# Feed-forward parts with block sums: the first and third sum of weight blocks by a plain load and an accumulating transfer

## The reference

```python
def _swiglu(x, wg, wu, wd):
    return (jax.nn.silu(x @ wg) * (x @ wu)) @ wd
```

## Time and profile before

| | |
|---|---|
| median of three runs | 1286.71 us (1285.36 to 1286.94) |
| the profiled execution's own time | 1287.52 us |
| its span, from the first to the last instruction | 1285.8 us |
| PE busy | 1268.0 us, 99% of the span |
| DVE busy | 909.5 us, 71% |
| ACT busy | 717.7 us, 56% |
| POOL busy | 130.6 us, 10% |
| moved by transfers | 252.84 MB, mean 197 GB/s |

### The profile page before, as it was taken

One profiled execution on the slowest core, in us unless ns is written; L12 is line 12 of the kernel. 1 busy time (PEld: TensorE's weight loads), 2 busy tenths in 40 slices (PEclk: granted clock), 3 DMA queues, 4 the chain that ended last, 5 costly groups with the idle time before them and its releaser, 6 DMA issues.

```text
span 1285.8 us, 17821 instructions
## 1 busy us (share of the span) xinstructions
PE 1268.0 (99%) x6941; PEld 1049.8 (82%) x6941; DVE 909.5 (71%) x1016; ACT 717.7 (56%) x952; POOL 130.6 (10%) x120
## 2 busy tenths in 40 slices
PE   8999999999999999999999999999999999999998
PEld 6887788888888888877788887888887887788886
DVE  4487776554876665766887866878866687887874
ACT  4344544445755555746746556555647655746553
POOL 3000099000450000020000000000000200000000
PEclk9999999999999999999999999999999999999999
DMA  9997486556465555562766354946264544675351
GB/s 336 351 402 243 141 284 215 192 185 208 127 224 181 187 191 195 192 209 66 254 206 228 98 189 155 327 132 229 82 229 132 165 147 132 219 272 188 108 175 70
DMA packets 164853, 252.84 MB, mean 197 GB/s; under 512 B 9336, under 2 KB 119220, under 8 KB 164788
## 3 DMA queue, kind: packets, MB, share of 16 engines
q1 hardware_dynamic: 161792, 243.28, 56.6%
q0 software_dynamic: 2624, 8.48, 1.7%
q10 hardware_dynamic: 372, 0.19, 0.1%
HBM read 248.73 MB, written 1.05 MB: 194 GB/s over the span
## 4 chain that ended last, share of the span: by engine, by line
PE 88%; ACT 5%; DVE 4%; SPq 1%; DMA 1%; issue 1%; DVEq 0%; ACTq 0%
PE ps L757 19%; PE ps L759 18%; PE ps L758 18%; PE ps L864 10%; PE ps L861 5%; PE ps L975 3%; PE ps L976 3%; PE ps L979 3%; PE ps L805 1%; PE ps L1362 1%; PE ps L797 1%; PE ps L798 1%; DMA raw<-in_conv_w_in 1%; PE ps L781 1%; ACT xT_pair L1611 1%; PE ps L1225 1%
## 5 line engine op out<-in xcount | busy, mean ns | idle before, releaser
L2171 DVE TENSOR_TENSOR w_lo<-raw,w_hi 128x2048 fp32r<-128x2048 f32 x150 | 344.0, 2298 | 92.9 <-ACT w_hi L1548 92.2
L1548 ACT ACTIVATE w_hi<-raw 128x2048 fp32r<-128x2048 f32 x150 | 285.9, 1910 | 117.9 <-PE ps L759 83.0
L757 PE MATMUL ps<-w_lo,hT_hi 128*128 128x512 f32 x400 | 157.0, 393 | 0.2
L864 PE MATMUL ps<-xT_pair,w_hi 128*128 128x512 f32 x576 | 157.2, 394 | 0.0
L758 PE MATMUL ps<-w_hi,hT_hi 128*128 128x512 f32 x400 | 155.9, 390 | 0.0
L759 PE MATMUL ps<-w_hi,hT_lo 128*128 128x512 f32 x400 | 155.8, 389 | 0.0
L757 PE MATMUL ps<-w_lo,xT_pair 128*128 128x512 f32 x356 | 141.5, 398 | 0.0
L759 PE MATMUL ps<-w_hi,xT_pair 128*128 128x512 f32 x356 | 138.9, 390 | 0.0
L758 PE MATMUL ps<-w_hi,xT_pair 128*128 128x512 f32 x356 | 138.7, 390 | 0.0
L864 PEld LDWEIGHTS ps<-xT_pair,w_hi 128*128 128x128 f32 x576 | 98.4, 189 | 13.2
L757 PE MATMUL ps<-xT_pair,w_hi 128*128 128x256 f32 x368 | 108.4, 294 | 0.2 <-DVE xT_pair L2577 0.2
(11 more groups left out here) (345 smaller groups left out, 2260.1 us busy)
## 6 DMA issues: line engine op xcount, KB each, us to landing
raw<-in_ffn_w_down SPq DMA_DIRECT2D x88, 512.0 KB, 4.4
raw<-in_ffn_w_gate SPq DMA_DIRECT2D x64, 512.0 KB, 4.0
raw<-in_ffn_w_up SPq DMA_DIRECT2D x64, 512.0 KB, 5.0
raw<-in_ffn_w_in SPq DMA_DIRECT2D x44, 512.0 KB, 4.6
raw<-in_conv_w_in SPq DMA_DIRECT2D x24, 512.0 KB, 9.9
arena<-in_ffn_w_up SPq DMA_DIRECT2D x24, 512.0 KB, 5.7
raw<-in_fox_w_in SPq DMA_DIRECT2D x24, 512.0 KB, 4.6
raw<-in_ffn_w_out SPq DMA_DIRECT2D x22, 512.0 KB, 4.1
```

Of the source, the lines that this page charges most:

```text
L757: pe.matmul(o, a_hi, b_lo, start=first, stop=False, skip_group_check=True)
L864: mm = pe.matmul(ps[:, bank, :].rearrange("p (s c) -> p s c", s=2), hi[:, cols[k]], xT_pair[:, :, 4 * u + k, :], start=False, stop=u == 1 ...
L1548: act.activation(w_hi[:, slot_of(n), :], raw[:, raw_slot(n), :], ACT.Copy).then_inc(hi_ready, 1)
L2171: dve.tensor_tensor(w_lo[:, slot_of(n), :], source(n), w_hi[:, slot_of(n), :].bitcast(F32), ALU.subtract).then_inc(raw_done, 1)
```

## The change

T1 and T3 are no longer formed by DVE. For T1 SP loads b_12 (the up columns) plainly into the buffer that becomes T1, and when it has landed, POOL issues a transfer of the gate block from the chip's main memory that adds to what is there. For T3 SP loads b_12 into a second buffer, and POOL issues a transfer that adds b_22. b_11, b_22 and b_21 are still loaded plainly. So a pair has five plain block loads (`L_X` and `L_Y` under T1 and T3, and `L_B22`, `L_B21`, `L_B11`) in place of four, and two accumulating transfers. `L_B11` comes last. T1 has a buffer of its own in `arena` (before: `tmp`), and two small buffers move. The semaphores of the four old block loads and of the sums are replaced or count anew.

```diff
-        b_11, b_12, b_22 = part(0, SLOT), part(2048, SLOT), part(4096, SLOT)
+        b_11, b_12, b_22, t_1 = [part(0 + i * SLOT, SLOT) for i in range(4)]
         b_21 = rows_flat[:, 2048:4096]
-        t_1, t_2 = [b[:, :, :].rearrange("p t d -> p (t d)") for b in (tmp, xn)]
+        t_2 = xn[:, :, :].rearrange("p t d -> p (t d)")
...
-                    dst = (b_11, b_12, b_22, b_21)[i].rearrange("p (k c) -> p k c", k=4)
-                    wd, k0 = ((gate, 0), (up, 0), (up, 4), (gate, 4))[i]
+                    dst = {L_B11: b_11, L_B22: b_22, L_B21: b_21, L_X: t_1, L_Y: b_12}[i].rearrange("p (k c) -> p k c", k=4)
+                    wd, k0 = {L_B11: (gate, 0), L_B22: (up, 4), L_B21: (gate, 4), L_X: (up, 0), L_Y: (up, 0)}[i]
...
                 sp.wait_ge(x_new, x_count(s - 1, 1, 1))
-                block(0, 0)
+                block(L_X, 0)
                 half_chunk(6, 2, 1)
-                block(1, 0)
+                block(L_Y, 0)
                 down_rows(7, 1)
-                block(2, 0)
+                block(L_B22, 0)
                 half_chunk(8, 3, 0)
-                block(3, 0)
+                block(L_B21, 0)
                 half_chunk(9, 3, 1)
+                block(L_B11, 0)
                 down_rows(10, 2)
                 down_rows(15, 3)
                 chunk(19, 6)
-                sp.wait_ge(raw_done, n + 13)
-                block(0, 1)
+                sp.wait_ge(raw_done, n + 15)
+                block(L_X, 1)
                 down_rows(21, 4)
                 sp.wait_ge(raw_done, n + 17)
-                block(1, 1)
+                block(L_Y, 1)
                 sp.wait_ge(raw_done, n + 18)
-                block(2, 1)
+                block(L_B22, 1)
                 sp.wait_ge(raw_done, n + 19)
-                block(3, 1)
+                block(L_B21, 1)
+                block(L_B11, 1)
                 down_rows(23, 5)
...
-                    act.wait_ge(sum_ok, 4 * i + {Q_T1: 1, Q_T2: 2, Q_T3: 3, Q_T4: 4}[q])
+                    act.wait_ge(sum_ok, 2 * i + (1 if q == Q_T2 else 2))
...
-                def sum_first(p):
-                    dve.wait_ge(quad_landed[0], 64 * (pair_no(s, p) + 1))
-                    if p:
-                        dve.wait_ge(raw_done, n + 14)
-                    else:
-                        dve.wait_ge(yT_ok, sums_count(s) + 1)
-                    dve.tensor_tensor(t_1, b_11, b_12, ALU.add).then_inc(sum_ok, 1)
...
                 def sum_second(p):
-                    dve.wait_ge(quad_landed[1], 32 * (pair_no(s, p) + 1))
-                    dve.wait_ge(sum_ok, 4 * pair_no(s, p) + 1)
+                    dve.wait_ge(t1_landed, sum_count(s, p))
+                    dve.wait_ge(block_landed[L_B22], block_count(s, p))
...
-                def sum_third(p):
-                    dve.wait_ge(sum_ok, 4 * pair_no(s, p) + 1)
-                    dve.tensor_tensor(b_12, b_12, b_22, ALU.add).then_inc(sum_ok, 1)
...
+            def add_blocks(s, p):
+
+                gate, up, _ = ffn_weights(s)
+                c0 = QUAD_CHUNK[p] * FCH
+                for plain, summed, dst, src in ((L_X, t1_landed, t_1, gate[:, 0:4, c0:c0 + 512]), (L_Y, t3_landed, b_12, up[:, 4:8, c0:c0 + 512])):
+                    pool.wait_ge(block_landed[plain], block_count(s, p))
+                    pool.dma_start(dst.rearrange("p (k c) -> p k c", k=4), src, accum_op=ALU.add).then_inc(summed, 16)
+
+            for s in (FFN2, FFN3):
+                for p in range(2):
+                    add_blocks(s, p)
             for i in range(FOX_H // 2):
...
+            for p in range(2):
+                add_blocks(FFN4, p)
```

More of the change, by code:

```diff
@@ L67 @@
            {22: Q_B21, 24: Q_B11, 25: Q_T1, 26: Q_T2, 28: Q_T3, 29: Q_B22, 30: Q_T4})
+L_B11, L_B22, L_B21, L_X, L_Y = range(5)
 QUAD_CHUNK = (4, 7)
@@ L286, in block_program @@
             "p (b h s) -> p b h s", b=2, h=2)
-        b_11, b_12, b_22 = part(0, SLOT), part(2048, SLOT), part(4096, SLOT)
+        b_11, b_12, b_22, t_1 = [part(0 + i * SLOT, SLOT) for i in range(4)]
         b_21 = rows_flat[:, 2048:4096]
-        t_1, t_2 = [b[:, :, :].rearrange("p t d -> p (t d)") for b in (tmp, xn)]
+        t_2 = xn[:, :, :].rearrange("p t d -> p (t d)")
         quad_src = {Q_B21: b_21, Q_B11: b_11, Q_T1: t_1, Q_T2: t_2, Q_T3: b_12, Q_B22: b_22, Q_T4: b_21}
-        s_1, u_2 = part(6144, 512), part(6656, 512)
+        s_1 = part(8192, 512)
+        u_2 = soft[:, :, :].rearrange("p a b -> p (a b)")
         s_5, u_3 = rows[:, 0, 0:512], rows[:, 0, 512:1024]
@@ L307, in block_program @@
         par_landed = sem("par_landed")
-        quarter_landed = [[sem(f"quarter_landed{q}{a}") for a in range(2)] for q in range(4)]
+        block_landed = [sem(f"block_landed{i}") for i in range(8)]
+        t1_landed = sem("t1_landed")
+        t3_landed = sem("t3_landed")
         part_landed = [sem(f"part_landed{i}") for i in range(NSLOT)]
@@ L369, in block_program @@
         up_tok0 = sem("up_tok0")
-        quad_landed = [sem(f"quad_landed{i}") for i in range(3)]
         e_ok = sem("e_ok")
@@ L457, in pair_no, with block_count, sum_count @@
             return 2 * SEVEN.index(s) + p
+        def block_count(s, p):
+            return 32 + 32 * (pair_no(s, p) + 1)
+        def sum_count(s, p):
+            return 16 * (pair_no(s, p) + 1)
         def row_count(s, c):
@@ L586, in block @@
                 def block(i, p):
-                    dst = (b_11, b_12, b_22, b_21)[i].rearrange("p (k c) -> p k c", k=4)
-                    wd, k0 = ((gate, 0), (up, 0), (up, 4), (gate, 4))[i]
+                    dst = {L_B11: b_11, L_B22: b_22, L_B21: b_21, L_X: t_1, L_Y: b_12}[i].rearrange("p (k c) -> p k c", k=4)
+                    wd, k0 = {L_B11: (gate, 0), L_B22: (up, 4), L_B21: (gate, 4), L_X: (up, 0), L_Y: (up, 0)}[i]
                     c0 = QUAD_CHUNK[p] * FCH
                     for h in (0, 2):
-                        sp.dma_start(dst[:, h:h + 2, :], wd[:, k0 + h:k0 + h + 2, c0:c0 + 512]).then_inc(quad_landed[max(i - 1, 0)], 16)
+                        sp.dma_start(dst[:, h:h + 2, :], wd[:, k0 + h:k0 + h + 2, c0:c0 + 512]).then_inc(block_landed[i], 16)
                 chunk(0, 0)
@@ L635, in load_quarter @@
                     for s in range(2):
-                        sp.dma_start(quarter_raw[q][a][:, :, s, :], ada_1[:, 4 * a:4 * a + 4, s, q * QUARTER:(q + 1) * QUARTER])                            .then_inc(quarter_landed[q][a], 16)
+                        sp.dma_start(quarter_raw[q][a][:, :, s, :], ada_1[:, 4 * a:4 * a + 4, s, q * QUARTER:(q + 1) * QUARTER])                            .then_inc(block_landed[2 * q + a], 16)
             def load_mod(q):
@@ L1135, in quarter_sums @@
             def quarter_sums(q, a):
-                pe.wait_ge(quarter_landed[q][a], 32)
+                pe.wait_ge(block_landed[2 * q + a], 32)
                 for g in range(4):
@@ L1756, in quad_hi @@
                 if q in (Q_B11, Q_B22, Q_B21):
-                    act.wait_ge(quad_landed[{Q_B11: 0, Q_B22: 1, Q_B21: 2}[q]], (64 if q == Q_B11 else 32) * (i + 1))
+                    act.wait_ge(block_landed[{Q_B11: L_B11, Q_B22: L_B22, Q_B21: L_B21}[q]], block_count(s, p))
+                elif q in (Q_T1, Q_T3):
+                    act.wait_ge(t1_landed if q == Q_T1 else t3_landed, sum_count(s, p))
                 else:
-                    act.wait_ge(sum_ok, 4 * i + {Q_T1: 1, Q_T2: 2, Q_T3: 3, Q_T4: 4}[q])
+                    act.wait_ge(sum_ok, 2 * i + (1 if q == Q_T2 else 2))
                 act.wait_ge(w_used, n - NSLOT + 1)
@@ L2453, in sum_second @@
                     dve.tensor_tensor(t_2, t_1, b_22, ALU.add).then_inc(sum_ok, 1)
-                def sum_third(p):
-                    dve.wait_ge(sum_ok, 4 * pair_no(s, p) + 1)
-                    dve.tensor_tensor(b_12, b_12, b_22, ALU.add).then_inc(sum_ok, 1)
                 def sum_fourth(p):
-                    dve.wait_ge(sum_ok, 4 * pair_no(s, p) + 2)
+                    dve.wait_ge(sum_ok, 2 * pair_no(s, p) + 1)
                     dve.wait_ge(raw_done, n + (23 if p else 12))
@@ L2494, in seven @@
                 turned(1, 2)
-                sum_first(0)
                 lo(8)
@@ L2501, in seven @@
                 turned(2, 0)
-                sum_third(0)
                 lo(11)
@@ L2515, in seven @@
                 lo(20)
-                sum_first(1)
                 turned(4, 3)
@@ L2522, in seven @@
                 turned(5, 0)
-                sum_third(1)
                 lo(24, 25, 26)
```

## The result

| | median of the runs | lowest to highest | profiled execution | its span |
|---|---|---|---|---|
| before, measured beside it | 1285.57 us (6 runs) | 1285.36 to 1286.94 | | |
| changed | 1307.55 us (6 runs) | 1305.06 to 1313.88 | 1306.50 us | 1304.7 us |

The changed kernel is slower: the ratio is 1.0167, with a 95% interval from 1.0153 to 1.0182, some 21.5 us. The sign and the mechanism are the predicted ones; the loss is a little over twice the predicted 9.9 us.

What follows compares the result with a forecast made beforehand. PE was taken as the bound, DVE's freed time worth 0; 3 x (2.8 + 0.5) = 9.9 us on the profiled 1287.52 gave 1297.4, less 0.81 to the median, 1296.6 us. Range 1285.5 to 1304, the forecast's own 1290 to 1304.

Steps and rivals of the forecast that it cites:

- the sum 3 x (2.8 + 0.5): Three FFN parts, each losing 2.8 us in pair 0 and 0.5 in pair 1: 9.9 us slower.
- c: Price of one accumulating transfer in plain 1 MB loads of 2.83 us: taken as 1.75, margins used up from 1.25.
- pair 1's 0.5: Loss per part ahead of the columns that need b_21 (unit 22): 0.5 us, range 0 to 1.0.
- What bounds the kernel: In the three changed parts PE sets the pace; taking 27.4 us of sums from DVE gains 0.
- The full stretch: From 624 to 652 us, at pair 0's block loads, DMA engines are full: mean share 1.05 at 371 GB/s.
- 5.66 c - 7.1: Pair 0's loss per part: landings of units 8 to 10 delayed 5.66 c, less a 7.1 us margin; 2.8 us.
- The shift of landings: Pair 0: both accumulating transfers are served before unit 8 lands, so units 8 to 10 land 5.66 c later.
- the rival *same time: No change, 1286.7 us: c below 1.4, or accumulating transfers give way to ring loads until units 8 to 10; chance 0.37.
- The sign that the prediction named: PE gap of 2 to 4 us ahead of unit 8 in each part, released by DVE's split of it.
- The margins of pair 0: Delay PE can stand from landing to need: unit 8 7.1 us, unit 9 7.1, unit 10 7.3 behind b_11.
- b_21's limit as 706.5: Pair 1: b_21 must land by 706.5 for PE's need at 709.82, landing near 699.5 before: margin 7.0 us.
- The upper bound: All three parts at c = 2 with 1.0 us for pair 1: 3 x 5.2 = 15.6 us, 1302.3 us.

Runs made afterwards that it cites:

- e4: The kernel before without DVE's sums for T1 and T3 and with nothing in their place: 1286.91 us, ratio 0.9999.
- e2: The changed kernel without POOL's transfers, T1 and T3 left as their plain blocks: 1286.1 us, ratio 0.9996.
- e1: The changed kernel with POOL's twelve accumulating transfers made plain loads of the same bytes: 1287.03 us, ratio 0.9998.
- e9: The changed kernel with two plain 1 MB loads from POOL in place of each accumulating transfer: 1307.11 us, ratio 1.0166.
- e7: e3 with the sum T2 moved on DVE to just ahead of the fourth sum: 1287.19 us, ratio 1.0003.
- e8: The changed kernel with pair 1's transfers made plain and pair 0's still accumulating: 1303.57 us, ratio 1.0134.
- e3: The changed kernel with pair 0's accumulating transfers held until unit 10 has landed, pair 1's second until unit 23 has: 1309.0 us, ratio 1.0157.

## Why the prediction was right in kind and too small

The path was right; the terms of its sum were too small. The step that failed is the sum 3 x (2.8 + 0.5): pair 0's 2.8 us a part measured 4.0 (c is 2.0, not 1.75), pair 1's 0.5 measured 1.3 (its limit had left out a split), and the clock, which the sum doesn't have, took 3.2 us in all.

- **What bounds the kernel; DVE's time is worth nothing.** Right. e4 gives it back without anything in its place: 0.9999.
- **SP's extra issues and the new order cost nothing.** Right: e2, and e1 with POOL's transfers plain.
- **The full stretch and c.** The mechanism was right, the size off. c was taken as 1.75, the middle of 1.5 and 2 (streams against reads), and is 2.0: 5.7 us against 2.8, and e9's two plain loads give the time of one accumulating. The term 5.66 c - 7.1 becomes 4.2 in place of 2.8 us per part; pair 0's gaps in the trace make 11.9 us in three parts, 4.0 in each. That the second load's worth of time is the read of the destination, as the working had it, no run shows by itself. The Trainium skill, "Collectives: The Full Stack", section "The bandwidth ceiling: the fold count and why AG ≠ RS ≠ AR", with its ratio of 1.93 for copying against adding, stood nearer than the middle did; the runs here agree with it at 2.0. The prediction's difference by it, 2.9 us over three parts, should read 3 x 5.66 x 0.18 = 3.1.
- **The shift of landings.** Right: 5.3 us measured at c = 1 (5.66 worked out), 10.5 at c = 2 (11.3). The ring was pushed back by nearly all of POOL's work, as even shares between the two queues would have it, so the rival *same time*, in which the ring would have been let through, is not what happened. It holds only by placing: e7. The sign that the prediction named came too: PE's gaps ahead of unit 8, 2.65, 3.41 and 4.00 us, are ended by DVE's split of it.
- **The margins of pair 0.** 7.1 us for unit 8 was right: e1 used 5.3 of it without a gap. Unit 7 was left out. DVE does its split, then `x_sums_lo()`, then `turned(1, 2)`, and only then can PE's products of unit 7 start, so it must land by about 644, and it landed at 644.7. That gap is 0.78 us, in FFN2 alone. It adds nothing to the sum: PE's need of unit 8 moved back by as much, and FFN2's two gaps of pair 0 together (3.43 us) are no longer than the one of FFN3 (3.41) or FFN4 (4.00).
- **Pair 1.** The step that took b_21's limit as 706.5 failed: it counted the columns' two halves behind ACT's split, but DVE also does `lo(21)` behind `turned(4, 3)`, 2.2 us, so the limit is 704.3 and the margin 4.8, not 7.0. The changed kernel, ACT's split of b_21 and, from DVE's timeline, `turned(4, 3)` and `lo(21)`, behind which the products at 715.03 begin:

```profile
709.56 1.92 ACT L1776 ACTIVATE w_hi<-rows 128x2048 fp32r<-128x2048 f32 x1 [4.39 <-DMA rows<-in_ffn_w_gate]
...
711.99 0.69 DVE L2429 TENSOR_TENSOR hT_lo<-ps,hT_hi 128x512 fp32r<-128x512 f32 x1 [5.70 <-ACT hT_hi L1799]
712.60 2.28 DVE L2186 TENSOR_TENSOR w_lo<-raw,w_hi 128x2048 fp32r<-128x2048 f32 x1
```

PE's need had moved back by 715.03 - 1.08 - 709.82 = 4.13 us, so the landing at 709.56 stands for 705.4 in the kernel before: inside the limit of 706.5, and 1.1 us outside that of 704.3. The prediction had b_21 land near 707. So a landing taken too late made up in part for a limit taken too late; with its own limit the measured landing would have cost nothing, and that its 0.5 is as near to the measured 1.3 as it is, is luck. It was priced at 0.5 us a part; by the gaps it is 1.3, 3.9 us in all in place of 1.5 (4.2 by e8).

- **Not in the sum at all: the clock.** Behind the two largest gaps PE ran some eight products at the lower level, 1.6 us each time, 3.2 us in the profiled execution.

The predicted 9.9 us, with 3.5 for pair 0, 2.4 for pair 1 and 3.2 for the clock, come to the 19.0 of the profiled execution; the 21.5 are those of all six, of which four took longer than it. The upper bound that the prediction worked out, c = 2 with 1.0 for pair 1, 15.6 us, was in effect the case that came, and it still lacked the clock.

## What to carry to other kernels

An accumulating DMA isn't a free add: here it took the engine time of two plain loads, so price it as two loads in the stretch where it runs, and ask there which later loads of other queues stand behind it. A margin is the time to the need of the whole chain behind a landing, so follow every instruction in the order of each engine between the landing and the consumer; of the two that were left out here, one, the low half of the input sums, merely stood ahead in DVE's list, and the other, unit 21's own split, PE needed. If such a transfer must stay, hold it until the urgent loads have landed and move what waits for it behind the work that PE needs; holding it alone was not enough (e3 against e7), and even both only broke even, because the engine that was relieved was not the bound (e4).

## What the runs showed of the hardware that was not expected

- The accumulating transfer showed a share above 1.0 at 207 GB/s of counted bytes (e3), where plain loads moved 379 at 1.06 (e1). The page's bytes of POOL's queue are the same for both, 21.06 MB, so bytes alone don't show the difference; the queue's share does (6.9% against 4.3%), and so do its packets: over the 2624 of the kernel before, 12 accumulating transfers make 528 each, 12 plain ones 272 (e1) and 12 pairs of plain ones 544 (e9).
- Issuing it held POOL 1.28 us, a plain one 0.75 us, with no consequence here.
- PE's granted clock fell to the lower level behind gaps of 2.42 (e9: 0.63 from 665 to 669 us), 2.99 (e8: 0.57 from 658 to 662), 3.41 and 4.00 us (changed kernel: 0.59 from 850 to 854, 0.57 from 1160 to 1164), 5.0 us (e3: 0.50 from 672 to 676), and did not behind 2.65 us in FFN2 of the changed kernel (1.00 from 660 to 668). So the length of the gap alone doesn't order these cases, and no run here settles what does.
